# A float32 decoder layer on one core: sums of the second down projection's weight blocks, made by accumulating DMA in the second up stage instead of by GpSimd in the first down stage

## What is computed

```python
D_MODEL, SEQ, D_FF = 1024, 512, 2816

def swiglu(x, w_gu, w_down):
    g, u = jnp.split(x @ w_gu, 2, axis=-1)
    return (jax.nn.silu(g) * u) @ w_down

x = x + 0.5 * rms_norm(swiglu(rms_norm(x, ffn1_norm_pre), ffn1_w_gu, ffn1_w_down), ffn1_norm_post)
x = x + rms_norm(merged @ w_out, mix_norm_post)          # merged: the attention branches of h @ w_in
x = x + 0.5 * rms_norm(swiglu(rms_norm(x, ffn2_norm_pre), ffn2_w_gu, ffn2_w_down), ffn2_norm_post)
```

## Time and profile before

| | us |
|---|---|
| median of 3 runs | 1160.94 (1158.41 to 1161.01) |
| the profiled execution | 1163.08 |
| its span, first to last instruction | 1161.4 |

### The profile page before, as it was taken

The page is one execution under the profiler, slowest core; times in us unless marked ns, Lnnn a source line. Parts: engine busy times, 40 slices in busy tenths (PEclk is TensorE's granted clock), DMA queues, the critical chain, the costliest instruction groups (busy, mean ns, idle before and its releaser), DMA issues.

```text
span 1161.4 us, 18860 instructions
## 1 busy us (share of the span) xinstructions
PE 1140.4 (98%) x7172; PEld 998.5 (86%) x7172; DVE 769.9 (66%) x1181; ACT 538.7 (46%) x992; POOL 144.5 (12%) x222
## 2 busy tenths in 40 slices
PE   9999999999998999999989999999999999999998
PEld 7889999988886888887967888888789999998886
DVE  5888888846527336445888353663589888888763
ACT  6255555532214312246778322334535555556543
POOL 0000000078467010000014100002000000000002
PEclk9999999999999999999999999999999999999999
DMA  7323333387976352453200222323222333335541
GB/s 218 109 66 96 99 103 108 109 303 211 376 254 202 93 144 74 143 177 114 76 3 2 73 75 107 127 73 109 73 73 74 109 108 108 108 109 200 200 162 72
DMA packets 145150, 146.46 MB, mean 126 GB/s; under 512 B 4660, under 2 KB 125660, under 8 KB 144044
## 3 DMA queue, kind: packets, MB, share of 16 engines
q1 hardware_dynamic: 137568, 114.31, 32.2%
q0 software_dynamic: 7408, 31.27, 7.7%
q10 hardware_dynamic: 112, 0.03, 0.0%
HBM read 132.76 MB, written 17.29 MB: 129 GB/s over the span
## 4 chain that ended last, share of the span: by engine, by line
PE 91%; DVE 4%; ACT 2%; issue 1%; DMA 0%; POOL 0%; SPq 0%; DVEq 0%; ACTq 0%
PE ps L2012 29%; PE ps L2119 28%; PE ps L2152 8%; PE ps L2178 6%; PE ps L2307 4%; PE ps L2602 4%; PE ps L2197 3%; PE ps L2586 2%; DVE ring_lo L1327 1%; PE ps L2438 1%; PE ps L2460 1%; PE ps L2574 1%; PE ps L2379 1%; PE ps L2369 1%; PE ps L2390 1%
## 5 line engine op out<-in xcount | busy, mean ns | idle before, releaser
L1327 DVE TENSOR_TENSOR ring_lo<-ring_raw,ring_hi 128x2048 fp32r<-128x2048 f32 (+1 forms) x60 | 146.6, 2444 | 124.8 <-ACT ring_hi L872 124.8
L872 ACT ACTIVATE ring_hi<-ring_raw 128x2048 fp32r<-128x2048 f32 (+1 forms) x60 | 112.9, 1884 | 206.4 <-PE ps L2012 72.9
L2012 PE MATMUL ps<-xn_hi,ring_hi 128*128 128x512 f32 x480 | 190.4, 397 | 2.4 <-DVE xn_lo L1352 2.3
L2012 PE MATMUL ps<-xn_lo,ring_hi 128*128 128x512 f32 x480 | 188.1, 392 | 0.0
L2012 PE MATMUL ps<-xn_hi,ring_lo 128*128 128x512 f32 x480 | 188.0, 392 | 0.0
L2119 PE MATMUL ps<-s_hi,ring_hi 128*128 128x256 f32 x512 | 144.9, 283 | 0.0
L2119 PE MATMUL ps<-s_lo,ring_hi 128*128 128x256 f32 x512 | 144.9, 283 | 0.0
L2119 PE MATMUL ps<-s_hi,ring_lo 128*128 128x256 f32 x512 | 144.9, 283 | 0.0
L2012 PEld LDWEIGHTS ps<-xn_hi,ring_hi 128*128 128x128 f32 x480 | 90.8, 189 | 21.6 <-issue 3.5
L2119 PE MATMUL ps<-x_hi,ring_lo 128*128 128x256 f32 x384 | 108.7, 283 | 0.0
L2119 PE MATMUL ps<-x_lo,ring_hi 128*128 128x256 f32 x384 | 108.7, 283 | 0.0
(11 more groups left out here) (339 smaller groups left out, 2359.3 us busy)
## 6 DMA issues: line engine op xcount, KB each, us to landing
ring_raw<-in_ffn_w_gu SPq DMA_DIRECT2D x86, 512.0 KB, 5.0
ring_raw<-in_w_in SPq DMA_DIRECT2D x42, 512.0 KB, 4.7
ring_raw<-in_ffn_w_down SPq DMA_DIRECT2D x40, 512.0 KB, 4.6
down_block<-in_ffn_w_down POOLq DMA_DIRECT2D x8, 1024.0 KB, 13.8
down_weight_sums<-down_block POOLq DMA_DIRECT2D x8, 1024.0 KB, 7.9
ring_raw<-down_weight_sums SPq DMA_DIRECT2D x16, 512.0 KB, 4.0
ring_raw<-in_w_out SPq DMA_DIRECT2D x8, 512.0 KB, 4.0
bias_rows_sparse<-bias_by_distance POOLq DMA_DIRECT2D x1, 2560.0 KB, 14.2
```

The source lines that it names most:

```text
L872: e = act.activation(dst, src, ACT.Copy)
L1327: e = dve.tensor_tensor(dst, src, f32(r), ALU.subtract)
L2012: e = pe.matmul(ps[:, 2 * (slot if pair is None else pair) + c, :], part(a, slot, k * 256 + c * P, P), xn[b][:, k, :], start=(k == 0 and i ...
```

## The change

The sums are no longer made by POOL in the first down stage. POOL now issues 20 transfers of 1 MB in the second up stage, each behind a wait for the one before it, all through one buffer `down_block` of 8 KB per partition: for each g a load of B11; then block B12 added to it by an accumulating transfer, stored as T1; B22 added, stored as T2; B21 added, stored as T4; then a load of B12, B22 added, stored as T3. That is 4 plain loads, 8 accumulating loads and 8 stores. They start after the first classic step (`w_used` at FFN2 + 1).

Without differences the sums are T1 = B11+B12, T2 = T1+B22, T4 = T2+B21, T3 = B12+B22. The signs are moved into the sums of the hidden state and into the closing of the banks: the same number of DVE instructions, eight of which (four calls, each made twice) become `scalar_tensor_tensor` with a factor of -1.

The buffer lies where chunks 14 to 17 of the hidden state go, which mixed steps 8 to 11 of the second up stage write. So DVE's loop is cut in two, after step 7, and in the second FFN DVE waits between the two for all eight stores. The cut is in the code of both FFNs, the wait only in the second.

```diff
-    blocks_sb = [at(f"down_block{i}", R + o * K, [4, S]) for i, o in enumerate((44, 52, 60, 78))]
+    block_sb = at("down_block", R + 28 * K, [4, S])
...
+            def add_blocks(dst, k_half, c, w_down, g, first=False):
+
+                src = by_k(w_down[(8 * g + 4 * k_half) * P:(8 * g + 4 * k_half + 4) * P, c * S:c * S + S])
+                if first:
+                    pool.dma_start(dst, src).then_inc(blocks_summed, 16)
+                else:
+                    pool.dma_start(dst, src, accum_op=ALU.add).then_inc(blocks_summed, 16)
+
+            def store_sum(which, src, g):
+                pool.dma_start(sums_dram[g, DOWN_SUMS.index(which)], src).then_inc(sums_stored, 16)
...
+            def sum_in_turn(w_down):
+
+                block = block_sb[:, :, :]
+                for g in range(2):
+                    add_blocks(block, 0, 0, w_down, g, first=True)
+                    wait_summed(1)
+                    for which, k_half, c in ((T1, 0, 1), (T2, 1, 1), (T4, 1, 0)):
+                        add_blocks(block, k_half, c, w_down, g)
+                        wait_summed(1)
+                        store_sum(which, block, g)
+                        wait_stored(1)
+                    add_blocks(block, 0, 1, w_down, g, first=True)
+                    wait_summed(1)
+                    add_blocks(block, 1, 1, w_down, g)
+                    wait_summed(1)
+                    store_sum(T3, block, g)
+                    wait_stored(1)
 
             rows_read(0)
             load_gain(g1_post)
-            load_blocks(0)
...
-            sum_blocks(0)
-            pool.wait_ge(sums_stored, 64)
-            load_blocks(1)
             pool.wait_ge(scratch_stored, 96)
-            sum_blocks(1)
 
             add_x(0)
-            pool.wait_ge(sums_stored, 128)
             pool.wait_ge(w_used, PROJ)
...
             add_x(1)
+            pool.wait_ge(w_used, FFN2 + 1)
+            sum_in_turn(w2_down)
             rows_read(1)
...
-                        e = dve.tensor_tensor(h_sum[1, g][:, :, :], a21, a22, ALU.add)
+                        e = dve.tensor_tensor(h_sum[1, g][:, :, :], a22, a21, ALU.subtract)
...
-                        e = dve.tensor_tensor(h_sum[2, g][:, :, :], h_sum[1, g][:, :, :], a11, ALU.subtract)
+                        e = dve.scalar_tensor_tensor(out=h_sum[2, g][:, :, :], in0=h_sum[1, g][:, :, :], scalar=-1.0, in1=a11,
+                                                     op0=ALU.mult, op1=ALU.subtract)
...
-                    dve.tensor_tensor(bank, bank, m5_sb[:, row, :], ALU.add).then_inc(down_closed, 1)
+                    dve.scalar_tensor_tensor(out=bank, in0=bank, scalar=-1.0, in1=m5_sb[:, row, :], op0=ALU.mult,
+                                             op1=ALU.subtract).then_inc(down_closed, 1)
...
-                with dve.Fori(1, MIXED // 2 - 1) as i:
-                    for u in range(2):
-                        mixed(i, u)
+                for i0, i1 in ((1, 4), (4, MIXED // 2 - 1)):
+                    if f and i0 == 4:
+                        dve.wait_ge(sums_stored, 128)
+                    with dve.Fori(i0, i1) as i:
+                        for u in range(2):
+                            mixed(i, u)
```

More of the change, by code:

```diff
@@ L400, in layer_kernel @@
     dve_chain = sem("dve_chain")
-    blocks_loaded, sum_made, sums_stored = sem("blocks_loaded"), sem("sum_made"), sem("sums_stored")
+    blocks_summed, sums_stored = sem("blocks_summed"), sem("sums_stored")
     h_summed, down_taken, down_closed = sem("h_summed"), sem("down_taken"), sem("down_closed")
@@ L738, in rows_read @@
                 pool.wait_ge(w_used, (FFN1, FFN2)[f] + UP)
-            def load_blocks(g):
-                for block_sb, (k_half, c) in zip(blocks_sb, ((0, 0), (0, 1), (1, 1), (1, 0))):
-                    k0 = 8 * g + 4 * k_half
-                    pool.dma_start(block_sb[:, :, :], by_k(w2_down[k0 * P:(k0 + 4) * P, c * S:c * S + S])).then_inc(blocks_loaded, 16)
-            def sum_blocks(g):
-                b11, b12, b22, b21 = [b[:, :, :] for b in blocks_sb]
-                t3, t1, t2, t4 = [sums_dram[g, i] for i in range(4)]
-                pool.wait_ge(blocks_loaded, 64 * (g + 1))
-                pool.tensor_tensor(b22, b22, b12, ALU.subtract).then_inc(sum_made, 1)
-                pool.wait_ge(sum_made, 4 * g + 1)
-                pool.dma_start(t3, b22).then_inc(sums_stored, 16)
-                pool.tensor_tensor(b12, b12, b11, ALU.subtract).then_inc(sum_made, 1)
-                pool.wait_ge(sum_made, 4 * g + 2)
-                pool.dma_start(t1, b12).then_inc(sums_stored, 16)
-                pool.tensor_tensor(b11, b22, b11, ALU.add).then_inc(sum_made, 1)
-                pool.wait_ge(sum_made, 4 * g + 3)
-                pool.dma_start(t2, b11).then_inc(sums_stored, 16)
-                pool.tensor_tensor(b21, b21, b11, ALU.subtract).then_inc(sum_made, 1)
-                pool.wait_ge(sum_made, 4 * g + 4)
-                pool.dma_start(t4, b21).then_inc(sums_stored, 16)
@@ new lines, in _, with wait_summed, wait_stored @@
+            summed, stored = [0], [0]
+            def wait_summed(n):
+                summed[0] += n
+                pool.wait_ge(blocks_summed, 16 * summed[0])
+            def wait_stored(n):
+                stored[0] += n
+                pool.wait_ge(sums_stored, 16 * stored[0])
+            def sum_in_turn(w_down):
[14 more added lines that the diff above has]
+                    wait_stored(1)
@@ L1517, in sum_h @@
                     if which == 4:
-                        e = dve.tensor_tensor(h_sum[4, g][:, :, :], a12, h_sum[2, g][:, :, :], ALU.subtract)
+                        e = dve.scalar_tensor_tensor(out=h_sum[4, g][:, :, :], in0=a12, scalar=-1.0, in1=h_sum[2, g][:, :, :],
+                                                     op0=ALU.mult, op1=ALU.subtract)
                     e.then_inc(h_summed, 1)
@@ L1534, in close_22 @@
                     dve.wait_ge(down_closed, 2 * row + 2)
-                    dve.tensor_tensor(bank, bank, u3_sb[:, row, :], ALU.add).then_inc(down_closed, 1)
+                    dve.scalar_tensor_tensor(out=bank, in0=bank, scalar=-1.0, in1=u3_sb[:, row, :], op0=ALU.mult,
+                                             op1=ALU.subtract).then_inc(down_closed, 1)
                 def close_12(row):
```

## The result

| | before | after |
|---|---|---|
| median, us | 1160.22 (1158.41 to 1161.01, 4 runs) | 1170.18 (1169.87 to 1171.35, 4 runs) |
| ratio to before | | 1.009 [1.0072, 1.0107] |
| profiled execution, us (its span) | 1163.08 (1161.4) | 1170.11 (1168.4) |
| mixed steps of the second up stage, start of the first and last product with s_hi and ring_hi, us | 886.0 to 1044.0 | 879.3 to 1050.6 |

The change makes the kernel 0.9% slower, by 10.0 us, against 9.4 forecast. (The profiled execution of before was 2.9 us above this median of before, so the two spans differ by 7.0 only.)

A forecast was written before the change was run, and what follows sets the result against it. PE, busy for 98% of the span, was taken to bound the kernel, any wait of it paid in full. A gain of 3.6 us and a loss of 13 gave +9.4: median 1160.9 to 1170.3 us, range 1157 to 1193.

The forecast's parts named there:

- The gain: First down stage and transition: without POOL's additions 3.1 + 0.5 = 3.6 us won, the transition lasting 15.0 us.
- The chain's length: Second up stage: the 20 transfers, one after another, take 157 us (133 to 173), SP's loads included.
- accumulating round: POOL's chain: an accumulating load takes 8.6 + 0.3 = 8.9 us until the next issue, eight take 71.2 us.
- store round: POOL's chain: a store takes 4.95 us until the next issue, eight take 39.6 us.
- the 23 us added for SP's loads: POOL's chain: about half of the engine time of some 12 SP loads falls on POOL's data, lengthening it by 23 us.
- the room: Second up stage: from the chain's start at 829.4 to its latest harmless end at 973.0 us, 143.6 us.
- The doubled data time: POOL's accumulating loads: 1 MB takes 6.0 us of data time in place of a plain load's 3.0.
- Which loss counts: Mixed steps: chain 13 us too late at DVE's wait, late loads 11 us; not additive, so the larger, 13 us, counts.
- The late loads: Mixed steps 0 to 7: SP's loads land late beside POOL's, 8 x (1.9 - 0.4) - 1.0 = 11 us (0 to 36).
- the 1.9 us: Mixed steps: the added landing time of an SP load beside one POOL transfer, from 7.2 against 5.3 us beside stores.
- the row of 5.0 us more: Profile row: SP's loads beside four of POOL's loads landed after 9.4 against 4.4 us; set aside for 1.9.
- Rival E: Mixed steps: SP's loads starve as queues alternate packets, each waiting out POOL's data; 32 us, 1189 us; chance 0.08.

The follow-up runs named there:

- the additions alone: The kernel before without POOL's four additions of g = 1 in the first down stage, its stores kept: 1157.69 us, ratio 0.9977.
- without the chain: The changed kernel without any of the 20 transfers and their waits; SP loads raw blocks in place of the sums: 1156.21 us, ratio 0.9966.
- half chain: The changed kernel with the ten transfers of g = 0 only; g = 1's products read raw blocks: 1158.37 us, ratio 0.9985.
- half chain later: The half chain started two one-block steps later, at about 847 instead of 823 us: 1159.91 us, ratio 0.9995.
- with the load: The half chain later, each accumulating transfer waiting for the same event as a load of SP's (DVE's low part): 1158.09 us, ratio 0.9977.
- behind the landing: The half chain later, each accumulating transfer waiting until a load of SP's has landed: 1167.41 us, ratio 1.0065.
- plain loads: The changed kernel with its eight accumulating loads as plain loads of the same size, order and waits kept: 1168.76 us, ratio 1.0068.
- ahead of the load: The half chain later, each accumulating transfer waiting for ACT's high part, so issued some 1.9 us before SP's load: 1172.14 us, ratio 1.008.
- the kernel with all eight sums: The changed kernel, chain started once POOL is free, three accumulating transfers of g = 1 issued just behind SP's loads: 1167.89 us, ratio 1.0056.

## Why the prediction was right, point by point

**Total.** 1170.3 us forecast, 1170.2 measured. That they agree to 0.1 us is luck. The 13 us of the sum were to come from the store's lateness, which cost nothing; in their place stand 13.3 us of late loads, which the sum had left out as the smaller loss.

**The gain, 3.6 us: right.** 15.0 us forecast for the transition, 15.02 measured; the wait of PE for L1327's low part is gone; the additions alone are worth 2.7 us. About 1 us more was won (4.8 without the chain), all of it ahead of the mixed steps; what it is was not tried. (In the profiled execution of before the granted clock was 0.88 in the windows behind both transitions, in after 1.00.)

**The chain's length: 157 us forecast, 152 measured** (822.98 to 975.0). An accumulating round was put at 8.9 us and takes 10.0 in the mean of eight (8.7 to 11.3); a store round at 4.95 and takes 6.0; the plain rounds at 5.9 and take 5.9. The rounds are thus 17.6 us longer than the 134.4 put for them, and the 23 us added for SP's loads stood for this delay in a lump, 5 us too much. The chain starts 6.4 us before the forecast's 829.4, but DVE's wait comes earlier by about as much: the room is 965.7 - 823.0 = 142.7 us, against 143.6. The doubled data time is confirmed: POOL's queue was busy 36.8 us of all engines more (10.8% of 1168.4 less 7.7% of 1161.4), and it had eight accumulating loads more and four plain ones fewer: (36.8 + 4 x 3.0) / 8 = 6.1 us an accumulating megabyte against 3.0 for a plain one. With the same eight as plain loads the queue's share is 8.9% of 1167.9 us, 22 us less than in after, 2.8 a transfer. "Collectives: The Full Stack" in the Trainium skill (section "The bandwidth ceiling: the fold count and why AG != RS != AR") says that the add of a ReduceScatter needs two source reads and so gets half the rate of a copy. That is said of collectives and not of a load into the core's own memory; the ratio measured here, 6.1 to 3.0, agrees with it.

**Which loss counts: the step that failed.** I took 13 us, the chain's lateness at DVE's wait, as the larger, and 11 us of late loads as the smaller. It is the other way round: the store would have been 975.0 - 965.7 = 9.3 us late, the late loads cost 13.3, and so the wait cost nothing. The "larger counts" was right (the kernel with the chain two steps later shows the case where the store decides).

**The late loads: right mechanism, term too small.** Forecast: 8 x (1.9 - 0.4) - 1.0. With the slack of the earlier trace rows (5.0 + 0.4 = 5.4 us to landing) and PE's 1.0 us, the landings read from each trace give the stage's loss to within 0.8 us, in the kernels where no store held DVE up:

| kernel | landings over 5.4 us, second half of the load | sum over 5.4, less 1.0 | stage less 158.0 |
|---|---|---|---|
| half chain | 8.1 | 1.7 | 1.7 |
| half chain later | 7.1, 5.8, 7.4 | 3.1 | 3.3 |
| with the load | 7.8, 5.6 | 1.6 | 1.8 |
| behind the landing | 7.7, 8.2, 7.7, 7.2, 8.3 | 11.1 | 11.1 |
| plain loads | 6.0, 7.7, 7.8, 7.9, 7.8, 7.8 | 11.6 | 11.4 |
| after | 5.5, 8.1, 10.5, 10.5, 7.3 | 13.9 | 13.3 |
| ahead of the load | 10.3, 9.9, 7.4, 10.3 | 15.3 | 16.1 |

So a slack read from one idle time of 0.42 us in the trace of before explains all seven, once their landings are known; the landings themselves it does not forecast. What was off was the 1.9 us: 8 x 1.5 = 12.0 us of the forecast stand against 14.9 of after, and no single value describes them: of its first eight loads four land as if alone (5.0 to 5.5) and two after 10.5. The 1.9 came from one load beside stores; the row of 5.0 us more, which I had set aside, was the nearer one for those two. One of the others fits no rule of order by its issue alone: the load of 893.1 lands after 8.1 us, 10 us behind an accumulating transfer and 1.2 us ahead of a store. The issue of its second half took 1.50 us in place of 0.44 and so ended behind the start of the store's, at 894.35; the half chain has a like case, 8.1 us with an issue of 1.35. Why the issue took so long is open.

**Rival E** (SP's packets take turns with POOL's, 32 us): the turns are there, the price was too dear. "DMA: Bandwidth & Descriptors" of the Trainium skill, section "Queues, rings and completion order", has each engine take a packet from each queue in turn. The trace agrees while both queues move: 238 packets of each in 3 us. A load issued just behind an accumulating transfer lands 5.5 us later than alone, near the 6.0 that E put for it; but E let all eight loads meet a transfer, and four of the eight landed as if alone. Turns alone don't give the order's effect either, since they say nothing of the time before the first packet, in which the second comer stands still. What holds it back there no run shows.

**Open:** why the two rhythms lock (15.05 us of step beside 15.2 us of round; with plain loads 12.4 beside 12.4 in the mean). The traces agree with this reading: a load that waits for POOL's transfer ends near POOL's landing, both sides then issue a few us later in the same order, and so on. It was read from two kernels, not tried by itself.

## What to carry to other kernels

Before you put transfers beside a stage, read how long its own loads may take (landing plus the idle time of the last engine in the loop), and sum what each load will be beyond that; the share of busy DMA engines did not tell it here (0.79 and 0.83 in two kernels with 0.04 and 7.0 us of idle PE). Let the filler transfer be issued right behind the critical load by waiting for the same event, never just ahead of it. It then takes longer itself (10.8 to 11.3 us against 8.9 to 9.3), and a filler with an end to meet can miss it by that, as the kernel with all eight sums did. Where there is a stage with slack, put it there instead.

## What the runs showed of the hardware

- Order of issue between two queues, in the mixed steps: a 2 x 512 KB load issued 0.4 to 1.2 us ahead of an accumulating 1 MB load landed in 5.1 to 5.5 us, one issued 1.1 to 1.5 us behind it in 9.9 to 10.7, 3.4 behind in 8.2 to 8.3, 4.4 behind in 7.7, about 7 behind in 5.0 to 6.1. Up to 1.8 us behind a plain load it was 7.2 to 7.9; behind a store 7.1 to 7.8 at 0.7 to 1.1 us, and 6.0 to 6.1 at 1.7 to 1.8. Alone it was 5.0 to 5.2.
- While both queues moved, each got as many packets as the other (238 and 238), although POOL's held 2 KB and SP's 512 bytes. The later of two transfers had its first packet late: 2.3 to 4.3 us after the issue of a load that has it after 1.05 alone.
- An accumulating 1 MB load into SBUF: 8.4 to 11.5 us to landing, 6.1 us of all engines' time against 3.0, and 1.3 us on POOL for its issue against 0.76 for a plain load and 0.57 for a store.
- An addition on POOL beside one on DVE: DVE's 128x2048 took up to 7.97 us in place of 2.3.
- In after the granted clock was 0.83 over the 20 us from 938 on, behind a pause of PE of 2.06 us and with one of 2.72 in them. In the kernel with all eight sums it was 0.71 over the 10 us from 968 on, which hold most of a pause of 7.8 us. After one of 1.72 us, at 907 in after, it stayed at 1.00.
